# Two output norms by halves of the tokens: the last units under them in two passes, the factor by a root and an inverse of columns

## The reference

```
def _rmsnorm(x, g):
    xf = x.astype(jnp.float32)
    return xf * lax.rsqrt(jnp.mean(xf * xf, axis=-1, keepdims=True) + NORM_EPS) * g.astype(jnp.float32)
...
x = x + _rmsnorm(y @ w_out[l], norm_mix_post[l]).astype(dt)          # first mixer's output norm
h = _rmsnorm(x, norm_ffn_pre[l]).astype(dt)
gate, up = jnp.split(h @ ffn_w_up[l], 2, axis=-1)
gate = _causal_dwconv(gate, ffn_conv_w[l], ffn_conv_b[l])
f = jax.nn.gelu(gate, approximate=True) * up
x = x + _rmsnorm(f @ ffn_w_down[l], norm_ffn_post[l]).astype(dt)     # first feed-forward stage's output norm
...
x = x + 0.5 * swiglu(rmsnorm(x, ffn1_norm), ffn1_w_gate, ffn1_w_up, ffn1_w_down)   # second block
x = x + hybrid_mixer(rmsnorm(x, mix_norm), ...)
x = x + 0.5 * swiglu(rmsnorm(x, ffn2_norm), ffn2_w_gate, ffn2_w_up, ffn2_w_down)
return rmsnorm(x, final_norm)
```

## Time and profile before

| | |
|---|---|
| median of 3 runs | 1667.12 us (1665.48 to 1675.3) |
| the profiled execution | 1676.78 us, span 1675.0 us |
| mean granted clock of TensorE | 0.986 of full |
| busy, share of the span | TensorE 98%, VectorE 49%, ScalarE 41%, POOL 16% |
| weight transfers | 148.5 MB, mean 89 GB/s |

### The profile page before, as it was taken

How to read it: one execution, slowest core, us unless ns; L and a number is a source line. 1 busy time by engine, 2 the same in 40 slices (tenths; PEclk the granted TensorE clock), 3 DMA queues, 4 the chain that set the end, 5 groups by cost and what they waited for, 6 DMA issues and landing times.

```text
span 1675.0 us, 22081 instructions
## 1 busy us (share of the span) xinstructions
PE 1643.0 (98%) x8648; PEld 1327.8 (79%) x8648; DVE 813.1 (49%) x1342; ACT 686.1 (41%) x1232; POOL 267.2 (16%) x225
## 2 busy tenths in 40 slices
PE   9999999899999999999999999999999999999997
PEld 6777777777888888877888888877877888888887
DVE  5566435556655542255444433347465544443333
ACT  7565546545443343245333333344133533333222
POOL 1221110301322220002222210000020032223000
PEclk9997989999999999999999999999999999999999
DMA  5221000222333333313332233332222233222332
GB/s 197 77 89 39 15 26 14 95 81 88 101 101 101 101 92 94 97 58 113 101 101 92 97 92 103 87 119 83 70 87 83 95 101 101 92 97 86 104 97 79
DMA packets 45399, 148.50 MB, mean 89 GB/s; under 512 B 5193, under 2 KB 8433, under 8 KB 45297
## 3 DMA queue, kind: packets, MB, share of 16 engines
q1 hardware_dynamic: 41760, 142.10, 27.2%
q10 hardware_dynamic: 3536, 5.00, 0.9%
HBM read 144.98 MB, written 2.10 MB: 88 GB/s over the span
## 4 chain that ended last, share of the span: by engine, by line
PE 92%; DVE 3%; ACT 3%; issue 1%; DMA 1%; POOL 0%; DVEq 0%; SPq 0%; ACTq 0%; POOLq 0%
PE bank L257 90%; PE bank L378 1%; DMA raw<-in_w_in 1%; ACT hi L998 0%; DVE lo L1661 0%; PE bank L430 0%; ACT sq L1017 0%; PE bank L438 0%; DVE acc L1677 0%; DMA raw<-in_w_out 0%; ACT L1028 0%; DVE hs L2362 0%; DVE B L2284 0%; DVE x L2429 0%; DVE y L2219 0%
## 5 line engine op out<-in xcount | busy, mean ns | idle before, releaser
L1661 DVE TENSOR_TENSOR lo<-raw,hi 128x512 fp32r<-128x512 f32 (+1 forms) x514 | 392.2, 787 | 603.6 <-ACT hi L998 603.3
L257 PE MATMUL bank<-xh,hi 128*128 128x512 f32 x1576 | 613.2, 396 | 6.5 <-issue 2.0
L257 PE MATMUL bank<-xh,lo 128*128 128x512 f32 x1576 | 603.5, 390 | 1.2 <-DVE lo L1661 1.2
L257 PE MATMUL bank<-xl,hi 128*128 128x512 f32 x1576 | 596.3, 390 | 0.0
L998 ACT ACTIVATE hi<-raw 128x512 fp32r<-128x512 f32 (+1 forms) x540 | 321.6, 616 | 458.2 <-PE bank L257 413.9
L257 PEld LDWEIGHTS bank<-xh,hi 128*128 128x128 f32 x1576 | 296.2, 188 | 79.7 <-issue 10.9
L257 PEld LDWEIGHTS bank<-xh,lo 128*128 128x128 f32 x1576 | 296.6, 188 | 64.6 <-DVE lo L1661 2.1
L257 PEld LDWEIGHTS bank<-xl,hi 128*128 128x128 f32 x1576 | 296.6, 188 | 63.4 <-issue 3.1
L257 PE MATMUL bank<-fH,hi 128*128 128x512 f32 (+1 forms) x550 | 210.1, 382 | 0.0
L257 PE MATMUL bank<-fH,lo 128*128 128x512 f32 (+1 forms) x550 | 209.3, 381 | 0.0
L257 PE MATMUL bank<-fL,hi 128*128 128x512 f32 (+1 forms) x550 | 209.3, 381 | 0.0
(11 more groups left out here) (387 smaller groups left out, 1147.2 us busy)
## 6 DMA issues: line engine op xcount, KB each, us to landing
raw<-in_ffn_w_up SPq DMA_DIRECT2D x88, 512.0 KB, 3.4
raw<-in_w_in SPq DMA_DIRECT2D x50, 512.0 KB, 3.5
raw<-in_ffn_w_down SPq DMA_DIRECT2D x48, 512.0 KB, 3.5
raw<-in_ffn_w_gate SPq DMA_DIRECT2D x44, 512.0 KB, 3.5
...
raw<-in_w_out SPq DMA_DIRECT2D x16, 512.0 KB, 3.4
...
```

Source lines behind the costliest of these rows:

```text
L257: return pe.matmul(out, w, x, start=start, stop=stop, skip_group_check=True)
L1661: dve.tensor_tensor(k.lo[i % CUT][:, 0:w], k.raw[u % RAW][:, at:at + w], k.hi[i % CUT][:, 0:w].bitcast(F), SUB).then_inc(k.cut_tail[i % 2], 1)
```

## The change

Two places are changed, the end of `out1` with the opening of A, and the end of A with the opening of B. The finale and the openings of the other stages keep their work; they only get new counts for semaphores.

- The last units (31 and 32 at the first place, the last down unit of 22 tiles at the second) run in two passes over the same weight pieces: first columns 0 to 255 of the tokens, then 256 to 511, each half into a bank of its own. The pieces are counted as used in the second pass only.
- The square and the `y` copy of these tiles are made by halves. At the first place VectorE also adds the sixth tile's squares by halves.
- `begin_sums`, `end_sums` with the seven matmuls on constants, and Ln and Exp go, at these two norms. In their place `row_sums` takes blocks of 128 tokens of `acc` and of the last square as weights and multiplies them by one column of ones: four matmuls give the sums of 256 tokens as two columns, tokens on partitions. ScalarE takes the square root (128x2), VectorE the reciprocal and then identity times these columns, a diagonal of 128x256, and `row_factor` multiplies ones by the diagonal, which spreads the factors over all partitions in a bank. VectorE multiplies `y` by that bank.
- Half 0's row sums stand behind tile 1 of the second pass and its factor behind tile 7. Half 1's stand in the opening, behind tiles 0 and 3 of half 0.
- The opening runs hi by xh and lo by xh for half 0 and then for half 1; hi by xl stays at full width.
- The cuts of pieces 68 to 71 and 202 to 207 are spread between the halves' steps on ScalarE and VectorE.

```diff
+COLS = [slice(0, 256), slice(256, 512)]
+FACTORS = {0: 0, 2: 1, 4: 2, 5: 3, 6: 4, 7: 5}
+HEADS = {0: 0, 1: 8, 2: 24, 3: 40, 4: 48}
+HALVES = {1: 0, 3: 2}
...
+def opening_by_halves(pe, k, S):
+    u0, i, v0 = S.unit, S.norm - 1, HEADS[S.normed]
+    outs, xh, xl = k.bank[0:3], k.xh, k.xl
+    part = lambda t, u, n: t[(2 * (u0 + u) + n // 4) % CUT][:, (n % 4) * 128:(n % 4) * 128 + 128]
+    def by_heads(h, n):
+        pe.wait_ge(k.head, v0 + 8 * h + n + 1)
+        for u, out in enumerate(outs):
+            if h == 0 and n % 4 == 0:
+                pe.wait_ge(k.cut_head, 2 * (u0 + u) + n // 4 + 1)
+            mm(pe, out[:, COLS[h]], part(k.hi, u, n), xh[n][:, COLS[h]], h == 0 and n == 0, False)
+    def by_tails(h, n):
+        for u, out in enumerate(outs):
+            c = 2 * (u0 + u) + n // 4
+            if h == 0 and n % 4 == 0:
+                pe.wait_ge(k.cut_tail[c % 2], c // 2 + 1)
+            mm(pe, out[:, COLS[h]], part(k.lo, u, n), xh[n][:, COLS[h]], False, False)
+    for h in range(2):
+        for n in range(4):
+            by_heads(h, n)
+            by_tails(h, n)
+            if h == 0 and n == 0:
+                row_sums(pe, k, i, 1)
+            if h == 0 and n == 3:
+                row_factor(pe, k, i, 1)
+        for n in range(4, 8):
+            by_heads(h, n)
+        for n in range(4, 8):
+            by_tails(h, n)
+    for n in range(8):
+        pe.wait_ge(k.tail, 8 * S.normed + n + 1)
+        for u, out in enumerate(outs):
+            m = mm(pe, out, part(k.hi, u, n), xl[n], False, n == 7)
+            if n % 4 == 3:
+                m.then_inc(k.used[(2 * (u0 + u) + n // 4) % CUT], 1)
...
-def begin_sums(pe, k, i):
-    b, n = k.uses.take(("norm", i), 6)
+def row_sums(pe, k, i, h):
+    b, n = k.uses.take(("norm", i, h), 7)
     room(pe, k, b, n)
     pe.wait_ge(k.both, i + 1)
-    mm(pe, k.bank[b], k.ones, k.acc[:, :], True, False)
-def end_sums(pe, k, i):
-    b, n = k.uses.at["norm", i]
-    pe.wait_ge(k.last_sq, k.last_sq_at[i])
-    mm(pe, k.bank[b], k.ones, k.sq[1][:, :], False, True).then_inc(k.full[b], 1)
-    pe.wait_ge(k.read[7], k.uses.n[7])
-    for _ in range(7):
-        mm(pe, k.bank[7][:, 0:CA], k.ones, k.cA[:, 0:CA], True, True)
+    if i == 1:
+        sem, v = k.added_at(1, 6)
+        pe.wait_ge(sem, v + h)
+    out, blocks = k.bank[b], [slice(256 * h + 128 * c, 256 * h + 128 * c + 128) for c in range(2)]
+    for c, at in enumerate(blocks):
+        mm(pe, out[:, c:c + 1], k.acc[:, at], k.ones[:, 0:1], c == 0, False)
+    pe.wait_ge(k.last_sq, HALVES[i] + h + 1)
+    for c, at in enumerate(blocks):
+        m = mm(pe, out[:, c:c + 1], k.sq[1][:, at], k.ones[:, 0:1], False, True)
+    m.then_inc(k.full[b], 1)
+def row_factor(pe, k, i, h):
+    b, n = k.uses.take(("factor", i, h), 6 + h)
+    room(pe, k, b, n)
+    pe.wait_ge(k.diagonal, HALVES[i] + h + 1)
+    mm(pe, k.bank[b][:, COLS[h]], k.ones, k.acc2[:, COLS[h]], True, True).then_inc(k.full[b], 1)
...
+def half_unit(pe, k, i0, tiles, out, xh, xl, h, between={}):
+    cs = COLS[h]
+    for t in range(tiles):
+        i, at = i0 + t // 4, slice(t % 4 * 128, t % 4 * 128 + 128)
+        if h == 0 and t % 4 == 0:
+            pe.wait_ge(k.cut_tail[i % 2], i // 2 + 1)
+        hi, lo = k.hi[i % CUT][:, at], k.lo[i % CUT][:, at]
+        mm(pe, out[:, cs], hi, xh[t][:, cs], t == 0, False)
+        mm(pe, out[:, cs], hi, xl[t][:, cs], False, False)
+        m = mm(pe, out[:, cs], lo, xh[t][:, cs], False, t == tiles - 1)
+        if h == 1 and (t % 4 == 3 or t == tiles - 1):
+            m.then_inc(k.used[i % CUT], 1)
+        if t in between:
+            between[t](pe, k)
+    return m
...
 def tensor_out1(pe, k):
-    for n in range(2, 8):
+    for n in range(2, 6):
         u = 25 + n
         b, m = k.uses.take(("out1", n), n % 4)
         room(pe, k, b, m)
-        piece(pe, k, 2 * u, k.bank[b], k.xh, k.xl, 0, False)
-        if n == 7:
-            begin_sums(pe, k, 1)
-        piece(pe, k, 2 * u + 1, k.bank[b], k.xh, k.xl, 4, True)
-    end_sums(pe, k, 1)
+        unit(pe, k, u, k.bank[b], k.xh, k.xl)
+    for h in range(2):
+        for n in (6, 7):
+            b, m = k.uses.take(("out1", n) if h else ("post", 1, n), n - 2 if h else n - 4)
+            room(pe, k, b, m)
+            between = {1: first_sums(1), 7: first_factor(1)} if h == 1 and n == 6 else {}
+            m = half_unit(pe, k, 2 * (25 + n), 8, k.bank[b], k.xh, k.xl, h, between)
+            if h == 0:
+                m.then_inc(k.full[b], 1)
...
+    if S.normed in (1, 2):
+        opening_by_halves(pe, k, S)
+    else:
+        opening(pe, k, u0, k.bank[0:3], k.xh, k.xl, k.head, k.tail, HEADS[4], 32)
...
-    for t in range(8 if S.then else 7):
+    for t in range(8 if S.then and not S.post else 7):
         b, n = k.uses.take((S.name, "down", t), 4 + t % 2)
         room(pe, k, b, n)
         for c in range(6):
             i = 2 * (u0 + 44 + 3 * t) + c
             piece(pe, k, i, k.bank[b], S.fH, S.fL, 4 * c, c == 5, S.f_tail if t == 0 else None, S.f0)
-            if S.post and t == 7 and c == 2:
-                begin_sums(pe, k, S.norm + 1)
     if S.post:
-        end_sums(pe, k, S.norm + 1)
+        for h in range(2):
+            b, n = k.uses.take((S.name, "down", 7) if h else ("post", 3, 7), 5 - h)
+            room(pe, k, b, n)
+            between = {1: first_sums(3), 7: first_factor(3)} if h else {}
+            m = half_unit(pe, k, 2 * (u0 + 65), 22, k.bank[b], S.fH, S.fL, h, between)
+            if h == 0:
+                m.then_inc(k.full[b], 1)
...
+def root(act, k, i, h):
+    b, _ = k.uses.at["norm", i, h]
+    act.wait_ge(*k.full_at(("norm", i, h)))
+    act.activation(k.rt[:, 2 * h:2 * h + 2], k.bank[b][:, 0:2], ACT.Sqrt, scale=1.0 / 1024,
+                   bias=k.eps[:, 0:1]).then_inc(k.read[b], 1)
...
+def post_half(act, k, i, n, h, y, gain):
+    cs, product = COLS[h], k.post_half(i, n, h)
+    b, _ = k.uses.at[product]
+    act.wait_ge(*(k.unit_done(k.post_unit(i, n)) if h else k.full_at(product)))
+    if h == 0:
+        act.wait_ge(*k.added_at(i, n - 2))
+    if n == 7:
+        act.activation(k.sq[1][:, cs], k.bank[b][:, cs], ACT.Square).then_inc(k.last_sq, 1)
+    else:
+        act.activation(k.sq[0][:, cs], k.bank[b][:, cs], ACT.Square).then_inc(k.squared, 1)
+    act.activation(y[n][:, cs], k.bank[b][:, cs], ACT.Copy, scale=k.col(gain, n)).then_inc(k.read[b], 1)
+def head_half(act, k, i, n, h, gain):
+    act.wait_ge(k.x_new, 8 * (HALVES[i] + h) + n + 1)
+    act.activation(k.xh[n][:, COLS[h]], k.xt[n][:, COLS[h]], ACT.Copy, scale=k.col(gain, n)).then_inc(k.head, 1)
 def scalar_out1(act, k):
-    log_table(act, k)
-    for n in range(8):
+    y, gain = k.y1, "norm_mix_post"
+    root_table(act, k)
+    for n in range(6):
         if n >= 2:
             cut_heads(act, k, 2 * (25 + n) + 6)
-        if n < 7:
-            post_tile(act, k, 1, n, k.unit_done(25 + n), k.y1, "norm_mix_post")
-        else:
-            post_last(act, k, 1, k.unit_done(32), k.read_at(("in1", 24)))
+        post_tile(act, k, 1, n, k.unit_done(25 + n), y, gain)
+    cut_heads(act, k, 68)
+    post_half(act, k, 1, 6, 0, y, gain)
+    post_half(act, k, 1, 7, 0, y, gain)
+    cut_heads(act, k, 69)
+    root(act, k, 1, 0)
+    cut_heads(act, k, 70)
+    post_half(act, k, 1, 6, 1, y, gain)
     act.wait_ge(k.got_x_again, 128)
-    post_heads(act, k, 1, "norm_ffn_pre")
+    for n in range(8):
+        head_half(act, k, 1, n, 0, "norm_ffn_pre")
+        if n == 0:
+            cut_heads(act, k, 71)
+        if n == 1:
+            post_half(act, k, 1, 7, 1, y, gain)
+        if n == 2:
+            cut_heads(act, k, 72)
+        if n == 3:
+            root(act, k, 1, 1)
+    for n in range(8):
+        head_half(act, k, 1, n, 1, "norm_ffn_pre")
...
+        cut_heads(act, k, 202)
+        post_half(act, k, 3, 7, 0, S.y, S.post)
+        root(act, k, 3, 0)
+        cut_heads(act, k, 204)
+        for n in range(8):
+            head_half(act, k, 3, n, 0, S.then)
+            if n < 3:
+                cut_heads(act, k, 205 + n)
+            if n == 3:
+                post_half(act, k, 3, 7, 1, S.y, S.post)
+                cut_heads(act, k, 208)
+            if n == 4:
+                root(act, k, 3, 1)
+        for n in range(8):
+            head_half(act, k, 3, n, 1, S.then)
...
+def diagonal(dve, k, i, h):
+    at, r = HALVES[i] + h + 1, k.rt[:, 2 * h:2 * h + 2]
+    dve.wait_ge(*k.read_at(("norm", i, h)))
+    dve.reciprocal(r, r).then_inc(k.inverted, 1)
+    dve.wait_ge(k.inverted, at)
+    dve.tensor_tensor(k.acc2[:, COLS[h]].rearrange("p (c t) -> p c t", c=2),
+                      k.ident.unsqueeze(1).broadcast_to([128, 2, 128]), r.unsqueeze(2).broadcast_to([128, 2, 128]),
+                      MUL).then_inc(k.diagonal, 1)
+def add_half(dve, k, i, n, h, y):
+    cs, at = COLS[h], 8 * (HALVES[i] + h) + n + 1
+    b, m = k.uses.at["factor", i, h]
+    if n == 0:
+        dve.wait_ge(*k.full_at(("factor", i, h)))
```

(85 more changed lines are left out.)

79 lines of the change are left out of this document (26 added, 53 removed).

## The result

Before: 1666.97 us median (1665.07 to 1678.79, 6 runs). After: 1692.66 us (1690.48 to 1696.28, 6 runs). Ratio 1.0144, 95% interval 1.0118 to 1.0171. The forecast was 1663.8 us, at most 1675; it missed by 29 us, and the loss is larger than everything that the change was said to touch (17.8 us).

The account below looks back on a forecast made before the run. TensorE, busy 98% of the span, was taken as the bound. Work and stalls of 34.8 us against 36.5 and 38.1 against 39.8 won 1.7 us each, 3.3 in all: 1663.8 us, own range 1661 to 1667, wider range 1656 to 1675.

Parts of the forecast that it names:

- What I cost at nothing: Both places: table loads, the wait at the next stage's column sum and TensorE's banks cost nothing; otherwise 0.5 us each.
- The whole touchable time is 17.8: Sums, waits and gaps at both places, 9.3 and 8.5 us, are all the change can touch: 17.8 us, 1.07%.
- TensorE's work: Matmuls, row sums and factors without stalls: 31.3 us at the first place, 35.7 us at the second.
- Stalls: First place: TensorE waits for the factor, cut pieces and heads, 3.5 us in all, 0.7 of it before the factor.
- lo 70: First place, opening: unit three waits for this piece, queued on VectorE behind adds and lo 69; 0.5 us stall.
- heads 5 to 7 of half 0: First place, opening: TensorE asks every 0.36 us, VectorE delivers every 0.79; stalls of 0.2 + 0.4 + 1.0 us.
- Second place: 35.7 us of work plus 2.5 of stalls make 38.1 against 39.8; unit 103's load comes late; 1.7 us won.
- Fed in time: Rival, both openings: VectorE's halves are shorter and the 6.0 us of stalls vanish, giving 1657.8 us; chance 0.15.
- The wait only moves: Rival, both places: row sum at 1.7 us and hand-overs of 0.1 us leave no gain, 1667 us; chance 0.20.
- The clock: Rival, openings: without idle passes the clock drops, 8.6 us lost per opening, 1672.4 or 1681.0 us; chance 0.12.
- Weight loads show: Rival, half-width matmuls: each of 420 also pays its load of 0.118 us, giving 1707 us; chance 0.01.
- A row sum of 0.1 us: Both places: lower bound of the row sum taken as 1.0 us; with bounds 1.7 and 0.1, gain 1.2 to 5.2.

Follow-up runs that it names:

- first experiment: The kernel before plus an unused four-column tile where the change allocates rt, so hi, lo and all behind begin 32 bytes later: 1694.76 us, ratio 1.017.
- second experiment: The changed kernel with rt allocated ahead of the pad, so every other tile lies where it lay before the change: 1666.15 us, ratio 0.9996.
- experiment 54: Not a run of its own: the words are the second experiment followed by a count, 54 half-width slots that take 6.47 us there.
- last experiment: The second experiment's kernel with, at the first place, the root and half 0's reciprocal and diagonal issued ahead of cut 68: 1669.16 us, ratio 1.0.

## Why the prediction was wrong

**The step that failed** is "What I cost at nothing". It listed table loads, a later wait and banks, and left out an edit of the diff: a tile is made in the middle of the layout. It costs 0.0067 us for each wide product with `xh` or `xl`. The three groups of these in the kernel before count 1576 each, 4728; 600 of them are the in projection's (25 units of 24). The other 4128 make 27.5 us from the out projection on; measured are 25.0 without the change (first experiment) and 1385.2 - 1360.6 = 24.6 with it. By the mean over all slots (0.0064 us longer) the 4128 make 26.4. What is left of the difference I put down to places where TensorE waits for others and a slower TensorE waits less; that is argued, not shown. The in projection adds 4.0 us: 25.0 and 4.0 make 29, and the medians of the first experiment stand 1694.76 - 1666.36 = 28.4 apart. No rival had a mechanism outside the two places, so the range ended where their mishaps did. "The whole touchable time is 17.8" was true of the instructions that the diff names, not of the kernel.

**TensorE's work**, forecast 31.3 us at the first place. Measured from the rows: 192 half-width slots of 0.118 us (54 of them from 342.54 to 348.92; in the second experiment 54 take 6.47 us, 0.120 each, so the 32 bytes did not hurt products of 256 columns) are 22.7, 24 wide ones at 0.2333 are 5.60. A row sum takes 349.73 - 348.92 = 0.81, and the slot of the product behind it is 0.08 longer: 0.89, where I took 1.0. The first factor takes 0.50 (0.32 to the next start, and 0.18 more in the slot behind it), the second, which did not wait, 0.43 (0.25 and 0.18), as forecast. 22.7 + 5.60 + 2 x 0.89 + 0.50 + 0.43 = 31.0.

**Stalls**, forecast 3.5 us there (the items as listed make 3.4). The idle time in a row counts from the modelled end of the product ahead, which is 0.28 us behind its start where the slot is 0.12: a listed stall is 0.16 us shorter than the delay, and short ones aren't listed at all (the slot from 360.57 to 360.93 holds a delay of 0.25 and no stall is shown). By starts: before the factor 0.88 (forecast 0.7); lo 70: none (forecast 0.5); heads 5 to 7 of half 0: from 359.90 to 363.57 are 3.67 us for the factor's 0.43 and 12 products, 1.42, so 1.8 (forecast 1.6); half 1 some 0.7 (forecast 0.6). Sum 3.4. It came out at 34.45 us against 34.8 forecast.

**Second place.** Before unit 103 TensorE lost 1.2 us (730.75 to 732.66 for six products, forecast 1.0), at tile 7 of half 0 735.67 to 738.60 is 1.1 us above its products and factor (forecast 0.9), in half 1 0.7 (0.6). 38.32 us against 38.1, and 38.07 in the second experiment, where the wide products of the opening are not slowed. The load of unit 103 went as said. SyncE's and ScalarE's rows in order of time, after:

```profile
727.49 0.33 SPq L2819 DMA_DIRECT2D raw<-in_ffn_w_gate  x1
...
731.02 0.63 ACT L1105 ACTIVATE hi<-raw 128x512 fp32r<-128x512 f32 x1 [0.89 <-DMA raw<-in_ffn_w_gate]
```

It is issued 13.9 us behind the start of the last unit and its first cut begins at 17.4, both as forecast, because `used` rises only in the second halves. VectorE's pace in the opening, the 0.79 us estimated from full-width rows, after:

```profile
361.64 0.41 DVE L2271 TENSOR_TENSOR y<-y,bank 128x256 f32<-128x256 f32 x1
...
362.43 0.41 DVE L2271 TENSOR_TENSOR y<-y,bank 128x256 f32<-128x256 f32 x1
```

**Rivals.** *Fed in time* fell by the waits above. *The wait only moves* fell for the change (3.3 us came out of it); in the last experiment a wait did only move, though not by this rival's prices. *The clock* fell: 1.00 in both openings. *Weight loads show* fell: 256-column products are 0.12 us apart over hundreds of rows, all with the same 128 rows of the array. The Trainium skill (TensorE: Matmul & The Clock Gate, "The mechanism" of part 3) lets a load overlap only where the row group differs; this trace does not agree. (The same section also names a background weight buffer as a case in which a load is pulled ahead; a load under the product before it is what the trace shows.) The rival's price for a load, 6.00 / 51 = 0.118 us, was the spacing of loads, not the length of one, which is 0.188 us in the page of the kernel before.

**The sum.** A row sum of 0.1 us, on the path three times, would add 2.7 us to the gain and make it 6.0, not the 5.2 that the prediction gives; nothing hung on it. "What I cost at nothing" held a second miss, a small one: the wait at the next stage's column sum grew. Before, and in the second experiment:

```profile
758.98 1.10 PE L257 MATMUL bank<-acc,cA 128*128 128x512 f32 x2 [1.40 <-DVE acc L1683]
```

```profile
751.99 1.10 PE L276 MATMUL bank<-acc,cA 128*128 128x512 f32 x2 [1.75 <-DVE acc L1832]
```

In that experiment the first place won 2.05 us and the second 1.71 (1.7 each forecast), and 0.35 of the 3.8 was lost again here; why VectorE's join of the sums comes later I leave open. So the mechanism inside the places held step by step, and that the total was 3.3 us as forecast, to within 0.1, is partly luck: errors of a few tenths cancelled. Of the 29 us by which the forecast missed, 26.5 are the layout's (1692.66 less the 1666.15 of the second experiment); the other 2.4 lie within the scatter of that experiment's runs (1661.42 to 1676.02).
